# Attention scores over 64 rows per component, on alternating row groups, with unpadded queries and one shared wait

## The chip, the core and the metric

One core of one Trainium2 chip (trn2) runs the whole program. The metric is the device time of one execution in microseconds (us); lower is better. PE is the matrix engine (TensorE), PEld its weight loads, DVE the vector engine, ACT the scalar engine, POOL GpSimd, SP the engine that issues most of the DMAs.

## The reference, cut to what matters

The program is one step of a two-layer decoder: a state-space layer (S5) with GLU and FFN, then differential attention over shared keys and values, and another FFN. The prompt has 1024 positions, the width is 1024, there are 8 heads, and each head has two components of 64 dimensions for queries and keys, and one value of 128. The change touches the attention of the prompt alone:

```python
def diff_attention(q, k, v, q_pos, k_pos, lam):
    s = jnp.einsum("bqhcd,bkhcd->bhcqk", q, k, preferred_element_type=jnp.float32) * (HEAD_DIM ** -0.5)
    mask = k_pos[None, :] <= q_pos[:, None]
    s = jnp.where(mask, s, NEG)
    p = jax.nn.softmax(s, axis=-1)
    w = p[:, :, 0] - lam * p[:, :, 1]
    return jnp.einsum("bhqk,bkhe->bqhe", w.astype(v.dtype), v)
```

Each component c has its own scores and its own softmax; the two are mixed into one weight matrix before the product with the values. Everything is float32.

## The kernel before, in words

The engines run hand-written instruction streams of their own, tied together by semaphores; nothing is reordered by a planner. Attention is 64 steps, numbered c = 0 to 63: head c // 8, query block i = c % 8 of 128 queries. A step works on n = 128 (i + 1) keys, so its size runs from 128 to 1024 within each head. `attention_steps` (L334) unrolls the first and last steps and loops over the rest, on every engine alike.

Data: `kh` holds the keys of a head, component 0 on partitions 0 to 63 and component 1 on partitions 64 to 127, two heads in turn (`par`). `qz` holds the queries twice per head: copy x has component x on its own 64 partitions and zeros on the other 64, so that a contraction over all 128 partitions of `kh` gives the scores of component x alone. The zeros are written once, by two memsets of POOL (L596, L598) before the first head; `load_head` (L459) brings keys and queries by DMA on SP's queue, and waits for `a_o` of the head before.

PSUM: `pair[0]` and `pair[1]` (two banks each) take the scores of component 0 and 1, `pair[2]` the transposes, banks 6 and 7 the outputs.

The order on each engine, in a step with scores c+1:

- PE (`step`, L1723): `scores(c+1, 0)`, `scores(c+1, 1)`, then `outputs(c-2)` (L1701, weights times values), at a head's end `values` (L1678, transposes of the next head's values), then `turn(c-1)` (L1712, transposes of the mixed weights). `scores` (L1686) for component x waits until the exponentials of component x of the step before have read `pair[x]` (`a_exp`), issues one float32 matmul for each 512 keys, and adds the causal mask of the last 128 keys by a bf16 matmul (`identb`, `maskb`), which signals `a_s`. A float32 matmul is two passes in the trace, each with its own weight load.
- DVE (`step`, L1302): `out_copy(c-3)`, the row maximum of component 0 of step c+1 (L1289), reciprocal and factor of step c (L1309, L1312), the mix of step c (L1317, `wmix`), then the row maximum of component 1 of step c+1.
- ACT (`step`, L835): the two exponentials of step c (L841), each of which needs its row maximum and signals `a_exp` after an accumulator read; the eviction of the transposes of step c-2 (L827), at a head's end `v_rows` (L820), the squares of step c-3 (L832).
- POOL and SP work beside it on the sample group's cached keys.

The waits of PE that set the order of the two components:

```python
if c:
    pe.wait_ge(a_exp, v * 2 + (x - 1))
```

Here v is the step's number, so component 0 waits for the first exponential of the step before, and component 1 for the second.

Earlier in the program, the S5 stage has float32 matmuls over 64 rows too (`outputs_s5`, L1530): two such matmuls on one row group, then one over 128 rows, in turn.

Of the kernel before, what the change touches and what calls it, by code (L numbers as in the profile page):

```python
# [20 lines left out]
F32 = mybir.dt.float32  # L21
# [8 lines left out]
P = 128  # L30
DM = 1024
KT = DM // P
SEQ = 1024
# [39 lines left out]
SEG1 = 108  # L73
# [7 lines left out]
def build(nc, d):  # L81
    ctx = ExitStack()
    with ctx:
        top = [((nc.sbuf_base + 31) // 32) * 32]

        def place(name, shape, dt, at=None):

            size = int(np.prod(shape[1:])) * (2 if dt == BF16 else 4)
            size = (size + 31) // 32 * 32
            if at is None:  # L90
                at = top[0]
                top[0] += size
                return nc.alloc_sbuf_tensor_at(name, shape, dt, offset=at)
            off = at[0]
            at[0] += size
            assert at[0] <= at[1], (name, at)
            return nc.alloc_sbuf_tensor_at(name, shape, dt, offset=off)

        def sem(name):
            return ctx.enter_context(nc.semaphore(name))  # L100
# [8 lines left out]
        identb = place("identb", [P, P], BF16)  # L109
# [106 lines left out]

        rf = [ACT_AT, HID_AT]
        kh = place("kh", [P, 2, SEQ], F32, rf)
        qz = place("qz", [P, 2, 2, SEQ], F32, rf)
        vT = nc.alloc_sbuf_tensor_at("vT", [P, 2, SEQ], F32, offset=RAW_AT)  # L220
        vtok = place("vtok", [P, 2, KT, P], F32, rf)
        prob = place("prob", [P, 2, 2, SEQ], F32, rf)
# [67 lines left out]
        d_o, d_sq, d_ssq, d_rs, d_fin = (sem(x) for x in ("d_o", "d_sq", "d_ssq", "d_rs", "d_fin"))  # L290
        op_ready, op_added = sem("op_ready"), sem("op_added")
        d_wp, d_row, d_ot = sem("d_wp"), sem("d_row"), sem("d_ot")
        q_zero, on_r, on_p = sem("q_zero"), sem("on_r"), sem("on_p")
        d_sc, d_hi, d_lo = sem("d_sc"), sem("d_hi"), sem("d_lo")
        passed = sem("passed")
        y_done, y_out = sem("y_done"), sem("y_out")
# [52 lines left out]
        def _(sp):  # L349
# [109 lines left out]
            def load_head(h, par):  # L459
                for c in range(2):  # L460
                    rows = slice(64 * c, 64 * c + 64)
                    for dst, src in ((kh[rows, par, :], k_v), (qz[rows, par, c, :], q_v)):
                        sp.dma_start(dst,
                                     src[ds(h, 1), c, :, :, 0:SEQ].rearrange("o m j t -> (o m) j t")
                                     ).then_inc(hd_in[par], 16)
                sp.dma_start(vT[:, par, :], d["vt"][ds(h, 1), :, 0:SEQ].rearrange("o e t -> (o e) t")
                             ).then_inc(hd_in[par], 16)
# [57 lines left out]
        @block.gpsimd  # L525
        def _(pool):
            g = nc.gpsimd

            def split(u, r, q, first):
                pool.wait_ge(w_in[r], q * 16 + 16)  # L530
                if not first:
                    pool.wait_ge(w_used, u - 2)
                    settle(pool)
                g.tensor_copy(w_hi[:, r, :], w_raw[:, r, :]).then_inc(w_hi_done, 1)  # L534
                pool.wait_ge(w_hi_done, u + 1)
                settle(pool)
                g.tensor_tensor(w_lo[:, r, :], w_raw[:, r, :], w_hi[:, r, :].bitcast(F32), ALU.subtract  # L537
                                ).then_inc(w_split, 1)

            def split_units(first, last):  # L540
                with pool.Fori(first // 4, last // 4) as b:
                    for r in range(4):
                        split(b * 4 + r, r, b, False)


            pool.wait_ge(s5_glob, 1)
            S4 = [P, PP, NI, NJ]
            G4 = [P, PP, NW, 16]
            c = Chain(pool, pool_chain)
            for q in range(PARTS):  # L550
                pr = slice(q * PP, q * PP + PP)
                G_re, G_im = G_r[q % 2], G_i[q % 2]
                if q:
                    pool.wait_ge(s5_h, q)

                def outer(dst, hi_t, lo_t):
                    return g.tensor_tensor(dst[:], bc(hi_t[:, pr, NW + NJ:NN], 3, S4),
                                           bc(lo_t[:, pr, NW:NW + NJ], 2, S4), ALU.mult)

                c.add(outer(CB, cosT, cosT))  # L560
                c.step(outer(CBt, sinT, sinT))
                c.step(g.tensor_tensor(CB[:], CB[:], CBt[:], ALU.subtract))
                c.add(outer(SB, sinT, cosT))
                c.step(outer(CBt, cosT, sinT))
                g.tensor_tensor(SB[:], SB[:], CBt[:], ALU.add).then_inc(s5_cs, 1)
                if q >= 2:
                    pool.wait_ge(s5_y, 8 * (q - 1))

                def cpow(dst, cc, aa):
                    return g.tensor_tensor(dst[:], bc(cc, 2, G4), bc(aa[:, pr, :], 3, G4), ALU.mult)  # L570

                c.add(cpow(G_re, c_in[:, 0, pr, :], A_re))
                c.step(cpow(G_t, c_in[:, 1, pr, :], A_im))
                g.tensor_tensor(G_re[:], G_re[:], G_t[:], ALU.subtract).then_inc(s5_g, 1)
                pool.wait_ge(s5_g, 2 * q + 1)
                c.add(cpow(G_im, ncr[:, pr, :], A_im))
                c.add(cpow(G_t, c_in[:, 1, pr, :], A_re))
                c.sync()
                g.tensor_tensor(G_im[:], G_im[:], G_t[:], ALU.subtract).then_inc(s5_g, 1)
                pool.wait_ge(s5_g, 2 * q + 2)  # L580
                if q == 0:
                    g.memset(ublk[0][:], 0.0).then_inc(s5_zero, 1)
                    pool.wait_ge(u_stored, 16)
                    c.step(g.memset(ublk[1][:], 0.0))
                    g.memset(TM[:], 0.0).then_inc(s5_zero, 1)

            pool.wait_ge(s5_y, 8 * (PARTS - 1))
            pool.wait_ge(s5_k, 4 * PARTS)
            for r in range(4):
                split(r, r, 0, True)  # L590

            split_units(4, SEG1)

            pool.wait_ge(kv_ready, 9 * KT // 2)
            pool.wait_ge(w_split, SEG1)
            g.memset(qz[64:P, :, 0, :], 0.0).then_inc(q_zero, 1)  # L596
            pool.wait_ge(q_zero, 1)
            g.memset(qz[0:64, :, 1, :], 0.0).then_inc(q_zero, 1)  # L598
            pool.wait_ge(q_zero, 2)

            with pool.Fori(0, NS // 2) as bb:
                for par in range(2):
                    for j in range(NPG):
                        if j == 0:
                            pool.wait_ge(kpg_in[0], bb * 64 + (32 * par + 32))
                        else:
                            pool.wait_ge(kpg_in[1], bb * 32 + (16 * par + 16))
                        settle(pool)
                        g.tensor_tensor(kpg[:, j, :], kpg[:, j, :], qb[:, par, :], ALU.mult).then_inc(d_mul, 1)

            pool.wait_ge(on_r, 1)
            for h in range(6):
                g.tensor_tensor(O[:, h], O[:, h], bc(orst[:, 8 * h:8 * h + 8], 2, [P, KT, P]), ALU.mult
                                ).then_inc(on_p, 1)
            split_units(SEG1, N_UNITS)
# [801 lines left out]
        def _(pe):  # L1417
            t_ = nc.tensor

            def mm(out, lhsT, rhs, start, stop):  # L1420
                return t_.matmul(out, lhsT, rhs, start=start, stop=stop)  # L1421
# [261 lines left out]
                    last = t_.transpose(pair[2][:, kb * P:(kb + 1) * P], vT[:, par, kb * P:(kb + 1) * P], ident[:])  # L1683
                last.then_inc(a_vt, 1)

            def scores(v, c, x):  # L1686

                i, par = c % 8, (c // 8) % 2
                if c % 8 == 0:
                    pe.wait_ge(hd_in[par], v * 5 + (80 * (c // 16 + 1) - 5 * c))  # L1690
                if c:
                    pe.wait_ge(a_exp, v * 2 + (x - 1))
                q = qz[:, par, x, i * P:(i + 1) * P]
                n = (i + 1) * P
                for at in range(0, n, 512):
                    end = min(at + 512, n)
                    last = mm(pair[x][:, at:end], q, kh[:, par, at:end], True, end < n)
                last = mm(pair[x][:, n - P:n], identb[:], maskb[:], False, True)
                last.then_inc(a_s, 1)

            def outputs(v, h, c):  # L1701

# [19 lines left out]

            def step(v, h, c):  # L1723
                if c != 63:
                    scores(v + 1, c + 1, 0)
                    scores(v + 1, c + 1, 1)
                if c >= 2:
                    outputs(v - 2, h if c % 8 >= 2 else h - 1, c - 2)
                if c % 8 == 7 and c != 63:
                    values(v + 1, h + 1, c + 1)  # L1730
                if c >= 1:
                    turn(v - 1, h + (2 if c % 8 == 7 and c != 63 else 1), c - 1)


            pe.wait_ge(kv_evicted, 9 * KT)
            pe.wait_ge(q_zero, 2)
            values(0, 0, 0)
            scores(0, 0, 0)
            scores(0, 0, 1)
            pe.wait_ge(d_qrow, 1)  # L1740
            attention_steps(pe, step)
            outputs(62, 7, 62)
# [179 lines left out]
```

## Time and profile before

| what | value |
|---|---|
| median of 3 executions | 2925.18 us (2923.54 to 2928.95) |
| profiled execution, first to last instruction (span) | 2914.3 us |
| PE busy in the span | 2601.8 us (89%) |
| DVE, ACT, POOL busy | 1225.4, 539.8, 801.2 us |
| attention of the prompt | about 1650 to 1952 us |

The profile gives no time of its own for the profiled execution beside the span. The span lies 10.9 us below the median, which is what lies around the first and the last instruction and the difference between executions. A timeline row gives the start, the duration, the engine and line, the operation with its output and inputs, and in brackets how long the engine had been idle before it and what released it. The end of a matmul is modelled, so its duration holds some latency, and starts are the better guide to how fast passes follow each other. PEclk is the clock that was granted to TensorE: 1.00 is 2.4 GHz, 0.50 is 1.2 GHz.

### The profile page before, as it was taken

How to read it: one execution, taken by the hardware profiler on the slowest of the kernel's cores; microseconds unless marked ns; L12 is line 12 of the kernel's file. 1: busy time of each engine (PE TensorE's matmuls, PEld its weight loads, DVE VectorE, ACT ScalarE, POOL GpSimd, SP SyncE). 2: the span in 40 equal slices, each digit the busy share in tenths (PEclk: the TensorE clock that was granted, in tenths of full speed). 3: DMA queues.
4: the chain of work that ended last, by engine and by line, in shares of the span. 5: the costliest groups of instructions: out<-in, count | busy, mean ns of one | idle time of the engine just before them, and what ended most of it. 6: DMA issues, size and time to landing. Idle time of an engine off the chain costs nothing.

```text
span 2914.3 us, 41251 instructions
## 1 busy us (share of the span) xinstructions
PE 2601.8 (89%) x16204; PEld 2460.8 (84%) x16204; DVE 1225.4 (42%) x2126; ACT 539.8 (19%) x1188; POOL 801.2 (27%) x439
## 2 busy tenths in 40 slices
PE   0468879999999999998999788879999999999997
PEld 0356679999999999998999566657999999999997
DVE  7876032433333333338114276663443333333237
ACT  2111131220000000003112255542120000000002
POOL 4163112223222332223323201130223232222230
PEclk9966589999999999999999899999999999999998
DMA  2423321111111111111322233223111111111101
GB/s 83 96 33 43 86 94 50 38 38 56 45 44 44 46 51 50 45 44 51 109 87 73 95 88 80 78 80 117 51 37 49 44 54 44 44 44 44 45 29 59
DMA packets 78896, 173.95 MB, mean 60 GB/s; under 512 B 18762, under 2 KB 41546, under 8 KB 78674
## 3 DMA queue, kind: packets, MB, share of 16 engines
q1 hardware_dynamic: 74994, 157.84, 18.6%
q10 hardware_dynamic: 3744, 13.74, 1.2%
q8 instruction: 131, 2.15, 0.3%
q14 instruction: 27, 0.22, 0.0%
HBM read 143.51 MB, written 25.69 MB: 58 GB/s over the span
## 4 chain that ended last, share of the span: by engine, by line
PE 82%; DVE 11%; issue 3%; DMA 2%; ACT 1%; SPq 1%; DVEq 0%; ACTq 0%
PE pair L1421 80%; DVE acc L913 2%; DVE act_lo L913 1%; DVE nmx L1289 1%; PE pair L1719 1%; DMA u<-U 1%; DVE tmp L941 1%; DVE X L913 0%; DVE diag L935 0%; DVE rho L1312 0%; DVE bbar L913 0%; DVE U L1081 0%; SPq L431 0%; DMA vT<-vt 0%; DVE wmix L1317 0%
## 5 line engine op out<-in xcount | busy, mean ns | idle before, releaser
L1421 PE MATMUL pair<-act_hi,w_hi 128*128 128x344 f32 x3264 | 1053.3, 323 | 43.8 <-DVE act_lo L913 33.8
L1421 PE MATMUL pair<-act_lo,w_hi 128*128 128x344 f32 x3264 | 1050.1, 322 | 8.3 <-issue 8.3
L1421 PE MATMUL pair<-act_hi,w_lo 128*128 128x344 f32 x3264 | 1049.8, 322 | 0.0
L1421 PEld LDWEIGHTS pair<-act_hi,w_hi 128*128 128x128 f32 x3264 | 621.6, 190 | 47.5 <-issue 36.1
L534 POOL CAST w_hi<-w_raw 128x1024 fp32r<-128x1024 f32 x180 | 196.0, 1089 | 1589.0 <-PE pair L1421 819.9
L1421 PEld LDWEIGHTS pair<-act_lo,w_hi 128*128 128x128 f32 x3264 | 619.6, 190 | 9.4 <-issue 9.4
L1421 PEld LDWEIGHTS pair<-act_hi,w_lo 128*128 128x128 f32 x3264 | 620.5, 190 | 0.0
L537 POOL TENSOR_TENSOR w_lo<-w_raw,w_hi 128x1024 fp32r<-128x1024 f32 x180 | 433.9, 2411 | 32.4 <-POOL w_hi L534 32.4
L913 DVE TENSOR_TENSOR tmp<-gate,pair 128x344 f32<-128x344 f32 x132 | 67.8, 513 | 762.8 <-ACT gate L745 762.8
L913 DVE TENSOR_TENSOR X<-X,pair 128x344 f32<-128x344 f32 x552 | 270.5, 509 | 199.8 <-PE pair L1421 199.7
L1421 PE MATMUL pair<-hid_lo,w_hi 128*128 128x344 f32 x1056 | 337.9, 320 | 0.0
L1421 PE MATMUL pair<-hid_hi,w_lo 128*128 128x344 f32 x1056 | 337.8, 320 | 0.0
L1421 PE MATMUL pair<-hid_hi,w_hi 128*128 128x344 f32 x1056 | 337.3, 319 | 0.0
L745 ACT ACTIVATE gate<-pair 128x344 f32<-128x344 f32 x132 | 60.4, 458 | 1200.0 <-PE pair L1421 1200.0
L1421 PEld LDWEIGHTS pair<-hid_hi,w_hi 128*128 128x128 f32 x1056 | 198.8, 188 | 0.0
L1421 PEld LDWEIGHTS pair<-hid_lo,w_hi 128*128 128x128 f32 x1056 | 198.5, 188 | 0.0
L1421 PEld LDWEIGHTS pair<-hid_hi,w_lo 128*128 128x128 f32 x1056 | 198.3, 188 | 0.0
L913 DVE TENSOR_TENSOR hid_lo<-tmp,hid_hi 128x344 fp32r<-128x344 f32 x132 | 164.7, 1248 | 73.7 <-ACT hid_hi L747 73.7
L1421 PE MATMUL pair<-kh,qz 128*128 128x512 f32 (+3 forms) x384 | 153.7, 521 | 30.4 <-ACT prob L841 29.4
L1421 PEld LDWEIGHTS pair<-kh,qz 128*128 128x128 f32 x384 | 65.6, 198 | 83.1 <-issue 54.3
L1289 DVE TENSOR_REDUCE nmx<-pair 128x1 f32<-128x256 f32 (+7 forms) x128 | 96.4, 753 | 76.8 <-PE pair L1421 76.7
L841 ACT ACTIVATE prob<-pair,nmx 128x256 f32<-128x256 f32 (+7 forms) x128 | 94.6, 740 | 95.8 <-DVE nmx L1289 94.8
(222 smaller groups left out, 2120.6 us busy)
## 6 DMA issues: line engine op xcount, KB each, us to landing
w_raw<-w SPq DMA_DIRECT2D x180, 512.0 KB, 3.5
kpg<-cache_k SPq DMA_DIRECT2D x16, 512.0 KB, 9.3
vpg<-cache_v SPq DMA_DIRECT2D x16, 512.0 KB, 4.2
X<-x_t SPq DMA_DIRECT2D x3, 1376.0 KB, 10.3
vt<-stage ACTq DMA_DIRECT2D x8, 516.0 KB, 4.7
y_t<-Y SPq DMA_DIRECT2D x3, 1376.0 KB, 5.4
ublk<-u SPq DMA_DIRECT2D x32, 128.0 KB, 5.2
z<-zblk SPq DMA_DIRECT2D x32, 128.0 KB, 3.3
```

The lines of the kernel that those rows point to most:

```text
L534: g.tensor_copy(w_hi[:, r, :], w_raw[:, r, :]).then_inc(w_hi_done, 1)
L537: g.tensor_tensor(w_lo[:, r, :], w_raw[:, r, :], w_hi[:, r, :].bitcast(F32), ALU.subtract).then_inc(w_split, 1)
L745: a.activation(gate[:, n, :], bank[2 * n][:, 0:CW], ACT.Silu).then_inc(gu_silu, 1)
L841: a.activation(prob[:, c % 2, x, 0:n], pair[x][:, 0:n], ACT.Exp, bias=nmx[:, c % 2, x:x + 1], accum_out=sums[:, c % 2, x:x + 1]).then_inc( ...
L913: return v_.tensor_tensor(out, a, b, op)
L941: return v_.scalar_tensor_tensor(out, view(X[:, k, cols]), gains[:, g, k:k + 1], view(R[:, cols]), ALU.mult, ALU.mult)
L1289: v_.tensor_reduce(nmx[:, c_ % 2, x:x + 1], pair[x][:, 0:n], axis=AXX, op=ALU.max, negate=True).then_inc(a_max, 1)
L1421: return t_.matmul(out, lhsT, rhs, start=start, stop=stop)
L1719: last = t_.transpose(pair[2][:, kb * P:(kb + 1) * P], wmix[:, c % 2, kb * P:(kb + 1) * P], ident[:])
```

## The change

The padded queries `qz` become `qh`, in the layout of `kh`: each component on its own 64 partitions, once. The two memsets and the semaphore `q_zero` with PE's wait for it go away. `scores` does both components in one call: it waits once, until both exponentials of the step before are done, then issues for each chunk of up to 512 keys the matmul of component 0 over partitions 0 to 63 and that of component 1 over partitions 64 to 127, and after all chunks the two mask matmuls, each of which signals `a_s`. The number of DMAs, the other engines' orders and their waits stay.

```diff
-        qz = place("qz", [P, 2, 2, SEQ], F32, rf)
+        qh = place("qh", [P, 2, SEQ], F32, rf)
...
-                    for dst, src in ((kh[rows, par, :], k_v), (qz[rows, par, c, :], q_v)):
+                    for dst, src in ((kh[rows, par, :], k_v), (qh[rows, par, :], q_v)):
...
-            pool.wait_ge(kv_ready, 9 * KT // 2)
-            pool.wait_ge(w_split, SEG1)
-            g.memset(qz[64:P, :, 0, :], 0.0).then_inc(q_zero, 1)
-            pool.wait_ge(q_zero, 1)
-            g.memset(qz[0:64, :, 1, :], 0.0).then_inc(q_zero, 1)
-            pool.wait_ge(q_zero, 2)
...
-            def scores(v, c, x):
+            def scores(v, c):
 
                 i, par = c % 8, (c // 8) % 2
                 if c % 8 == 0:
                     pe.wait_ge(hd_in[par], v * 5 + (80 * (c // 16 + 1) - 5 * c))
                 if c:
-                    pe.wait_ge(a_exp, v * 2 + (x - 1))
-                q = qz[:, par, x, i * P:(i + 1) * P]
+                    pe.wait_ge(a_exp, v * 2)
                 n = (i + 1) * P
                 for at in range(0, n, 512):
                     end = min(at + 512, n)
-                    last = mm(pair[x][:, at:end], q, kh[:, par, at:end], True, end < n)
-                last = mm(pair[x][:, n - P:n], identb[:], maskb[:], False, True)
-                last.then_inc(a_s, 1)
+                    for x in range(2):
+                        rows = slice(64 * x, 64 * x + 64)
+                        mm(pair[x][:, at:end], qh[rows, par, i * P:(i + 1) * P], kh[rows, par, at:end], True, end < n)
+                for x in range(2):
+                    mm(pair[x][:, n - P:n], identb[:], maskb[:], False, True).then_inc(a_s, 1)
...
                 if c != 63:
-                    scores(v + 1, c + 1, 0)
-                    scores(v + 1, c + 1, 1)
+                    scores(v + 1, c + 1)
...
-            pe.wait_ge(q_zero, 2)
             values(0, 0, 0)
-            scores(0, 0, 0)
-            scores(0, 0, 1)
+            scores(0, 0)
```

## Rows read from the trace of the kernel before

**Rows 1.** Page, costliest groups: scores, row maxima and exponentials.
```profile
L1421 PE MATMUL pair<-kh,qz 128*128 128x512 f32 (+3 forms) x384 | 153.7, 521 | 30.4 <-ACT prob L841 29.4
L1289 DVE TENSOR_REDUCE nmx<-pair 128x1 f32<-128x256 f32 (+7 forms) x128 | 96.4, 753 | 76.8 <-PE pair L1421 76.7
L841 ACT ACTIVATE prob<-pair,nmx 128x256 f32<-128x256 f32 (+7 forms) x128 | 94.6, 740 | 95.8 <-DVE nmx L1289 94.8
```

**Rows 2.** Busy time by window over the attention: PE, PEld, DVE, ACT, POOL, clock, DMA.
```profile
1648.00:1952.20 304.20, 263.35 (x1383) 181.18 (x1383) 214.21 (x395) 167.98 (x449) 56.42 (x26) 0.95 0.29 87
```

**Rows 3.** Instructions by line, 1648 to 1950 us: the mix.
```profile
L1317 DVE SCALAR_TENSOR_TENSOR wmix<-prob,rho 128x128 f32<-128x128 f32 (+7 forms) x63 | 57.0, 905 | 2.5
```

**Rows 4.** Waits between engines, 1648 to 1950 us: total, times, longest.
```profile
ACT prob L841 <- DVE nmx L1289: 92.5, 87, 4.2
DVE nmx L1289 <- PE pair L1421: 76.7, 50, 14.8
...
PE pair L1421 <- ACT prob L841: 29.4, 26, 3.1
```

**Rows 5.** Timeline of one step with 896 keys and the next.
```profile
1820.24 1.09 DVE L1289 TENSOR_REDUCE nmx<-pair 128x1 f32<-128x896 f32 x1 [1.32 <-PE pair L1421]
...
1821.70 1.02 DVE L1317 SCALAR_TENSOR_TENSOR wmix<-prob,rho 128x768 f32<-128x768 f32 x1
...
1822.63 1.08 DVE L1289 TENSOR_REDUCE nmx<-pair 128x1 f32<-128x896 f32 x1
...
1823.15 1.88 PE L1421 MATMUL pair<-kh,qz 128*128 128x512 f32 x4
...
1823.75 1.01 ACT L841 ACTIVATE prob<-pair,nmx 128x896 f32<-128x896 f32 x1 [1.28 <-DVE nmx L1289]
...
1824.65 0.19 ACT L841 ACTIVATION_READ_ACCUMULATOR prob<-pair,nmx 128x1 f32 x1
...
1824.87 0.22 PE L1421 MATMUL pair<-maskb,identb 128*128 128x128 bf16 x1
...
1824.92 1.96 PE L1421 MATMUL pair<-kh,qz 128*128 128x512 f32 x4
1825.12 1.23 DVE L1289 TENSOR_REDUCE nmx<-pair 128x1 f32<-128x1024 f32 x1 [1.15 <-PE pair L1421]
```

**Rows 6.** Timeline at the end of that head.
```profile
1828.83 0.22 PE L1421 MATMUL pair<-maskb,identb 128*128 128x128 bf16 x1
...
1831.65 0.77 PE L1421 MATMUL pair<-kh,qz 128*128 128x128 f32 x2 [2.60 <-ACT prob L841]
...
1832.32 2.76 PE L1421 MATMUL pair<-vtok,wT 128*128 128x128 f32 x12
...
1837.79 0.21 ACT L841 ACTIVATION_READ_ACCUMULATOR prob<-pair,nmx 128x1 f32 x1
```

**Rows 7.** Busy time by window around the gap in rows 6.
```profile
1828.06:1831.48 3.42, 0.98 (x10) 0.76 (x8) 2.66 (x4) 1.18 (x3) 0.00 (x0) 0.99 0.00 0
1831.48:1834.89 3.41, 3.24 (x15) 3.16 (x16) 1.87 (x4) 0.72 (x2) 0.00 (x0) 0.51 0.00 0
```

**Rows 8.** Timeline of PE in the S5 outputs.
```profile
346.05 0.82 PE L1421 MATMUL pair<-ublk,TM 128*128 128x136 f32 x2
346.80 0.82 PE L1421 MATMUL pair<-H,G_re 64*128 64x136 f32 x2
...
348.00 0.59 PE L1421 MATMUL pair<-ublk,TM 128*128 128x136 f32 x1
```

**Rows 9.** Busy time by window in the S5 outputs.
```profile
332.00:360.00 28.00, 28.00 (x87) 20.73 (x87) 0.00 (x0) 2.78 (x7) 13.35 (x8) 0.50 0.43 162
```

**Rows 10.** Timeline of the first head's start: a memset, and PE's first transposes.
```profile
1631.73 1.80 POOL L598 MEMSET qz<- 64x2048 f32 x1
...
1647.98 1.94 PE L1683 MATMUL pair<-ident,vT 128*128 128x128 f32 x8 [15.16 <-DMA vT<-vt]
```

More of the change, by code:

```diff
@@ L292, in build @@
         d_wp, d_row, d_ot = sem("d_wp"), sem("d_row"), sem("d_ot")
-        q_zero, on_r, on_p = sem("q_zero"), sem("on_r"), sem("on_p")
+        on_r, on_p = sem("on_r"), sem("on_p")
         d_sc, d_hi, d_lo = sem("d_sc"), sem("d_hi"), sem("d_lo")
```

## The prediction

> **What bounds the kernel now.** I read the page's groups first, then the busy times of the attention stage, the waits between engines there, and the timeline of one head. The scores are 384 passes [rows 1]; outside the attention nothing changes, so the question is about the 302 us from 1650 to 1952, or 37.8 us for each of the 8 heads. In that stage PE is busy 87% of the time and DVE 70% [rows 2], which looks like a stage that PE bounds. But the waits run in a ring: ACT waits 92.5 us for row maxima, DVE 76.7 us for scores, PE 29.4 us for exponentials [rows 4]. The timeline shows why PE is still well fed. The passes of component 0 with 1024 keys start at 1823.15, while the second exponential of the step before runs from 1823.75; those of component 1 start at 1824.92, just after that exponential was read out at 1824.84. Then DVE takes the first maximum (1825.12) beside component 1's passes [rows 5]. The two components work in turns: PE on one, DVE and ACT on the other. The two waits, one for each component, are what allows it.
>
> **The ring after the change.** Now both components wait for the second exponential of the step before, and both masks, whose signals release the maxima, come after all chunks. So nothing of a step's scores lies beside the maxima and exponentials of the step before, and the ring is closed once in a step: scores of both, maximum 0, factor and mix of the step before, maximum 1, exponential 1, and back. Outputs and transposes, 16 passes in the largest step, lie beside DVE's part.
>
> Its length without the passes: from maximum 0 (1820.24) to the release of the next component's passes (1824.92) is 4.68 us for 896 keys, of which 1.09 + 1.02 + 1.08 + 1.01 are the two maxima, the mix and the exponential, and 0.48 are the rest [rows 5]. From the start of four passes (1823.15) to the maximum (1825.12) is 1.97; the passes take 1.72 of it, as the mask that follows starts at 1824.87. That leaves 0.25 for mask and signal, and makes one pass of 512 columns 0.43 us. So a step has 0.73 us of fixed parts. For the seven steps of a head with 256 keys and more:
> - maxima: 96.4 / 8 = 12.05 us per head, less two of about 0.28 for 128 keys [rows 1] = 11.5;
> - mixes: 57.0 / 8 = 7.1 [rows 3], less that of 1024 keys, which falls into the next head's first step (1.3, estimated from 1.02 for 768 keys), = 5.8;
> - exponentials of one component: 94.6 / 16 = 5.9 [rows 1], less 0.4 = 5.5;
> - fixed: 7 x 0.73 = 5.1.
>
> Together 27.9 us. A head's first step goes another way: the outputs, the transposes of new values and `v_rows` stand ahead of its exponentials. It takes now from 1831.65 to the next release at about 1838.1, 6.4 us [rows 6], and goes on as it is, since the new passes (128 keys) are short. **A head without passes of its other seven steps: 34.3 us**, against 37.8 with everything now. This is the number that decides.
>
> **The passes.** A float32 matmul is two passes. Written so, the queue has component 0 first and second, then component 1 first and second, then the next chunk. If a pass can run beside one of the other row group but passes start in order, only the second of one pair lies beside the first of the next: one chunk takes 3 pass times where it took 4, two full chunks 5 where they took 8. For 256 to 1024 keys, with 0.43 us for 512 columns: 0.64, 0.96, 1.28, 1.49, 1.71, 1.92, 2.13 = 10.1 us per head. One after another it would be 14.9, and as two full halves 7.5; no row shows two row groups at once, so these are the bounds. I take the middle form, because in the trace passes always start in order.
>
> The Trainium skill (TensorE: Matmul & The Clock Gate, Part 3) says that matmuls on different row groups run at the same time, starting about 4 ns apart; by it as it stands, the sum would go by the 7.5, which is 2.6 us per head or 21 us in all below mine. No run so far shows it.
>
> **The change between 64 and 128 rows.** S5 is the nearest place: there a cycle of four passes over 64 rows and two over 128, 136 columns each, takes 348.00 - 346.05 = 1.95 us [rows 8] at the half clock [rows 9]. Six such passes are 6 x 0.227 = 1.36 (136/512 of 0.43, doubled). So two changes cost 0.59 us at 1.2 GHz. Each score step gets two (into the 64 rows, back for the mask). The clock may scale all of it or none, 0.3 to 0.6 a step; at the full clock I take 0.3: 7 x 0.3 = 2.1 us per head.
>
> The Trainium skill (TensorEngine Tiling (Array Packing), Key Properties) says that a change of tiling mode drains TensorE. It speaks against this change, and the trace agrees, with 0.59 us for two.
>
> **At the full clock**: 34.3 + 10.1 + 2.1 = 46.5 us, 8.7 more than 37.8, for 8 heads **70 us** more.
>
> **The clock.** Now PE has one long gap in a head, 2.60 us from 1829.05 to 1831.65 [rows 6], and the granted clock falls from 0.99 to 0.51 right behind it, for the next 3.4 us [rows 7]. After the change the ring leaves PE a gap in every step. With 1024 keys DVE's and ACT's part is 5.2 us and outputs and transposes about 2.0; the gap is 3.2. With 512 keys it is 3.4 less 0.7, or 2.7. So five steps of each head (512 keys and more) have a gap at least as long as the one that costs the clock today. And mixed passes over 64 rows did not bring it back in S5: 28 us with PE marked busy throughout, at 0.50 [rows 9]. I take half clock for the passes from 640 keys up (+7.25), half of that for 512 (+0.64), 0.3 for changes and masks in each of five steps (+1.5), and about as much for the slower small steps (+1.5): 10.9 us per head, **87 us**. Outputs and transposes at half clock (3.4 us for the largest) still fit beside DVE's part.
>
> **Nothing or next to nothing.** The memsets took 1.80 us each on POOL, done at 1633.5, while PE waited for the first values until 1647.98 [rows 10]: no gain, the DMA covers it. Loads keep their number, bytes and waits; a longer stage gives them more time. Fewer waits on PE save nothing where PE waits anyway.
>
> **Sum**: 70 + 87 = 157 us. Against the span 2914.3 that is 3071; the median lies 10.9 above the span, and nothing around it changes, so **3083 us**.
>
> **The rivals.**
> - *The row groups run one after another* (the array takes no second row group, or the instruction does not ask for it: the change does not do what it says). For it: no row shows two row groups at once. Against it: weight loads already run beside passes (PE and PEld together are busy for longer than the stage) [rows 2], so the array does take work in parts. The Trainium skill's rule above speaks against it too. The time: 34.3 + 14.9 + 2.1 = 51.3 at full clock, plus a clock term of 12.8 for the passes of five steps and 3 for the rest: 67, 29 more per head, 234 in all: about 3160. Chance 0.15.
> - *The clock holds.* If the gaps are broken by late outputs, PE stays at 2.4 GHz and the change costs the ring alone: 70 us, or with full concurrency 49: 2974 to 2995. For it: 0.95 granted now [rows 2]; against it: five gaps as long as the one that dropped it. Chance 0.16.
> - *PE was the bound, and the change relieves it.* 15.4 us of passes per head (with 128 keys) fall to 10.5 or 7.7, less 8 x 0.3 for changes: 2.5 to 5.3 saved per head, 20 to 42 in all, about 2895. It decides only if the ring is shorter than PE's work, that is if the part without passes is under 37.8 - 10.1 - 2.1 = 25.6 us per head. It is 34.3, so even passes of no length would win only 1.4 us per head after the changes. Chance 0.03, and 0.01 for a time that cannot be told from now.
> - The forecast, ring plus clock, has 0.65; its own range is 3040 to 3130, from full concurrency (34.3 + 7.5 + 2.1 + about 8, or 51.9 per head, +113) to half clock in all steps (+16 per head for the clock, +198).
>
> The range for 8 in 10 is 2990 to 3165: it leaves out the faster rival, the lower part of the second one and the upper part of the first. A measurement of this kernel can tell about 0.2% from no change; faster by more than that 0.03, within it 0.01, slower 0.96.
>
> **What would show it.** The profile after should show: PE's passes of both components starting after the read of the second exponential, never beside it; maximum 0 starting only after both components' passes; DVE and PE idle in turn, with PE's share in the stage well under 87%; a period of 8 to 10 us with 1024 keys, where a step now takes under 5 on average; component 1's first pass starting with component 0's second; a granted clock of 0.6 to 0.8 over the stage; and a stage of about 460 us in place of 302. Passes that start all one after another make the first rival true, a clock above 0.9 the second. I am wrong altogether if maximum 0 starts before component 1's last pass, which would mean that the two components still work in turns.

## The result, and the profile after

| kernel | median | runs | against before (95% interval) |
|---|---|---|---|
| before | 2925.78 us | 2923.54 to 2928.95 | |
| changed | 3006.77 us | 3003.06 to 3013.87 | 1.0281 (1.0263 to 1.0300) |

The change costs 81 us. The forecast was 3083, with a range of 2990 to 3165: the sign and the mechanism hold, the size is half of what was forecast, and 3007 lies below the 3040 to 3130 that the prediction gave for ring and clock as it had sized them. The profiled execution has a span of 3001.2 us, 86.9 more than before. Its time is 1.9 us above its span; so most of the 10.9 us that lie between span and median before are no fixed part: the execution profiled before was one of the fastest.

The groups that answer to [rows 1], from the page of the changed kernel:

```profile
L1414 PE MATMUL pair<-kh,qh 64*128 64x512 f32 (+3 forms) x384 | 109.6, 690 | 123.5 <-ACT prob L834 123.5
L1282 DVE TENSOR_REDUCE nmx<-pair 128x1 f32<-128x256 f32 (+7 forms) x128 | 96.4, 754 | 182.5 <-PE pair L1414 182.5
```

The 384 passes are busy for 109.6 us in place of 153.7: the two row groups overlap, as the starts of the passes show further down. But the idle time ahead of them grew from 30.4 to 123.5 us, all of it waiting for exponentials. The maxima take what they took (96.4) and wait 182.5 us in place of 76.8.

The stage by the window view, which answers to [rows 2] (PE, PEld, DVE, ACT, POOL, clock, DMA):

```profile
1648.00:2038.00 390.00, 254.18 (x1383) 168.63 (x1383) 208.39 (x395) 167.30 (x447) 55.78 (x26) 0.81 0.24 69
```

It ends 86 us later. PE is busy for 254 us, 9 less than before, in a stage that is much longer: 65% of it in place of 87%. DVE has 208 of 390. No engine is near its limit. The granted clock is 0.81 on the mean, where it was 0.95; the prediction expected 0.6 to 0.8, and a stage of about 460 us.

Waits between engines in that stage, which answer to [rows 4]:

```profile
DVE nmx L1282 <- PE pair L1414: 182.5, 64, 17.0
ACT prob L834 <- DVE nmx L1282: 172.7, 102, 5.3
...
PE pair L1414 <- ACT prob L834: 123.5, 50, 7.0
```

All three edges of the ring are longer, PE's more than four times. This is the ring that the prediction described. In the timeline, the step with 1024 keys that answers to [rows 5]:

```profile
1833.02 0.19 ACT L834 ACTIVATION_READ_ACCUMULATOR prob<-pair,nmx 128x1 f32 x1
...
1833.27 2.58 PE L1414 MATMUL pair<-kh,qh 64*128 64x512 f32 x8 [1.86 <-ACT prob L834]
...
1835.78 0.40 PE L1414 MATMUL pair<-maskb,identb 128*128 128x128 bf16 x2
...
1835.97 2.28 PE L1414 MATMUL pair<-vtok,wT 128*128 128x128 f32 x10
1836.11 1.22 DVE L1282 TENSOR_REDUCE nmx<-pair 128x1 f32<-128x1024 f32 x1 [3.77 <-PE pair L1414]
...
1837.70 1.15 DVE L1310 SCALAR_TENSOR_TENSOR wmix<-prob,rho 128x896 f32<-128x896 f32 x1
...
1838.76 1.22 DVE L1282 TENSOR_REDUCE nmx<-pair 128x1 f32<-128x1024 f32 x1
...
1840.02 1.11 ACT L834 ACTIVATE prob<-pair,nmx 128x1024 f32<-128x1024 f32 x1 [1.44 <-DVE nmx L1282]
...
1841.27 0.77 PE L1414 MATMUL pair<-kh,qh 64*128 64x128 f32 x4 [2.37 <-ACT prob L834]
```

Read it as a chain. The second exponential of the step before is read out at 1833.21, the passes of both components follow at 1833.27, maximum 0 comes after all of them (DVE had been idle for 3.77 us), then the mix, maximum 1, exponential 1, and the next passes at 1841.27. One turn of the ring is 8.00 us; over the heads, turns of this size take 7.35 us where the clock stays up and up to 9.21 where it does not. No pass lies beside an exponential of its own ring, and in the 2.37 us before 1841.27 PE has nothing to do.

### The profile page after: what moved, and what is told of

The parts are those of the page before. It is cut to its first block, busy times and chain, and to the rows that moved or that the text cites. A ratio compares the mean times of both kernels' runs of the same rounds, so it can differ in the third digit from the quotient of the medians.

```text
span 3001.2 us, 41241 instructions
## 1 busy us (share of the span) xinstructions
PE 2592.1 (86%) x16204; PEld 2448.3 (82%) x16204; DVE 1219.3 (41%) x2126; ACT 540.2 (18%) x1188; POOL 796.9 (27%) x437
## 4 chain that ended last, share of the span: by engine, by line
PE 79%; DVE 12%; issue 4%; DMA 2%; ACT 2%; SPq 1%; DVEq 0%; ACTq 0%
PE pair L1414 78%; DVE nmx L1282 3%; DVE acc L906 1%; DVE act_lo L906 1%; DMA u<-U 1%; DVE wmix L1310 1%; DVE tmp L934 0%; DVE rho L1305 0%; PE pair L1713 0%; DVE X L906 0%; DVE diag L928 0%; DVE bbar L906 0%; ACT prob L834 0%; SPq L431 0%; DVE U L1074 0%
## 5 line engine op out<-in xcount | busy, mean ns | idle before, releaser
L1414 PE MATMUL pair<-kh,qh 64*128 64x512 f32 (+3 forms) x384 | 109.6, 690 | 123.5 <-ACT prob L834 123.5
L1414 PEld LDWEIGHTS pair<-kh,qh 64*128 64x128 f32 x384 | 40.8, 236 | 164.1 <-ACT prob L834 132.8
L1282 DVE TENSOR_REDUCE nmx<-pair 128x1 f32<-128x256 f32 (+7 forms) x128 | 96.4, 754 | 182.5 <-PE pair L1414 182.5
L602 POOL TENSOR_TENSOR kpg<-kpg,qb 128x1024 f32<-128x1024 f32 x16 | 37.2, 2349 | 348.1 <-DMA kpg<-cache_k 348.1
```

The source lines that it names most:

```text
L1282: v_.tensor_reduce(nmx[:, c_ % 2, x:x + 1], pair[x][:, 0:n], axis=AXX, op=ALU.max, negate=True).then_inc(a_max, 1)
```

## The experiments

Times and ratios are each kernel's own against the kernel before on the same chip. The kernels were timed on several chips, where the kernel before has medians of 2923.5 to 2925.8 us, so a difference between two of them holds some 2 us of that.

A time is for the whole program, and part of what separates these kernels lies behind the attention, in instructions that no edit touches. The changed kernel and the one with work in PE's gaps, each split by the window view (columns as in [rows 2]) at the last pass of the attention's outputs:

```profile
1652.20:2050.20 398.00, 260.54 (x1433) 174.81 (x1432) 210.83 (x400) 171.98 (x457) 55.78 (x26) 0.82 0.23 66
2050.20:3001.20 951.00, 906.65 (x5767) 893.84 (x5765) 348.52 (x602) 116.45 (x236) 240.24 (x140) 0.97 0.16 51
```

```profile
1652.00:2024.20 372.20, 290.00 (x1573) 172.27 (x1572) 212.62 (x400) 171.97 (x457) 56.25 (x26) 0.94 0.25 70
2024.20:2958.10 933.90, 896.83 (x5767) 884.67 (x5765) 348.56 (x602) 116.43 (x236) 240.52 (x140) 0.98 0.16 52
```

The same 5767 passes follow the attention in both, and take 17 us less in the second. In the feed-forward stage behind the attention of the first, PE pauses four times, for 1.6 to 2.1 us, where nothing in the profile holds it back ("issue"), and the clock falls to half at each pause. The kernel before has such pauses too; this is the first, from its timeline:

```profile
2305.14 0.42 PE L1421 MATMUL pair<-act_lo,w_hi 128*128 128x344 f32 x1 [2.06 <-issue]
```

Seven of the twelve kernels have all four, five have none. It goes with the kernel, not with the chip: the seven have the same number of passes in the attention (1433), the five have more or fewer. Whether that decides it, and how, is open. So what an edit does to the attention is read from this table, one trace for each kernel; the execution profiled of the kernel before was one of its fastest, so up to 10 us of a distance to it can be the difference between executions.

| kernel | attention, first pass of scores to last of outputs (us) | behind it (us) | pauses |
|---|---|---|---|
| before | 315.0 | 949.6 | 4 |
| changed | 398.0 | 951.0 | 4 |
| own waits back | 354.1 | 949.9 | 4 |
| shared wait alone | 371.6 | 949.3 | 4 |
| all but the row groups | 480.5 | 946.5 | 4 |
| both maxima first | 322.7 | 948.1 | 4 |
| work in PE's gaps | 372.2 | 933.9 | 0 |
| component after component | 394.4 | 944.1 | 4 |
| without the masks | 388.1 | 933.2 | 0 |
| both maxima first, small filler | 317.9 | 928.1 | 0 |
| the same, padded queries | 355.4 | 928.0 | 0 |
| the same, component after component | 320.0 | 929.8 | 0 |

**Own waits back, 64 rows kept.**

```diff
-            def scores(v, c):
+            def scores(v, c, x):
...
-                    pe.wait_ge(a_exp, v * 2)
+                    pe.wait_ge(a_exp, v * 2 + (x - 1))
+                rows = slice(64 * x, 64 * x + 64)
...
-                for x in range(2):
-                    mm(pair[x][:, n - P:n], identb[:], maskb[:], False, True).then_inc(a_s, 1)
+                mm(pair[x][:, n - P:n], identb[:], maskb[:], False, True).then_inc(a_s, 1)
```

> The changed kernel with its unpadded 64-row passes, but the two components one after the other again, each with its own wait and its mask right behind it. Theory (the shared wait and the masks behind both components close a ring in every step): the turns come back, PE works on one component while DVE and ACT work on the other, and maximum 0 starts beside the passes of component 1. What stays is two more changes of row mode a step on a PE that was 87% busy: 2935 to 2975 us. Rival (what costs is the 64-row mode itself, its changes and a lower clock): there are twice as many changes here, so it stays at 3007 or goes above it.

Measured 2957.07 us, ratio 1.0117 (1.0098 to 1.0136): 50 us less than the change, in the range of the theory. Both components, 512 keys, PE's timeline:

```profile
1829.14 1.12 PE L1414 MATMUL pair<-kh,qh 64*128 64x512 f32 x2
1830.20 0.23 PE L1414 MATMUL pair<-maskb,identb 128*128 128x128 bf16 x1
1830.36 1.12 PE L1414 MATMUL pair<-kh,qh 64*128 64x512 f32 x2
1831.41 0.23 PE L1414 MATMUL pair<-maskb,identb 128*128 128x128 bf16 x1
1831.48 0.44 PE L1414 MATMUL pair<-vtok,wT 128*128 128x128 f32 x2
```

Two passes of 512 columns take 2 x 0.43 = 0.86 us at the full clock, and the masks start 1.06 and 1.05 us behind the first of them: 0.2 us for the change from 64 to 128 rows. The other way, the pass starts 0.16 us behind the mask, where passes over 128 rows start 0.05 us behind it [rows 5]: 0.11 us for the change back. The turns are back. What stays of the loss, 31 us, has the size of the changes, 64 steps with two of each or 40 us at most, on a PE that had little to spare; but the granted clock is lower too (0.86 from 1648 to 1952 us, where it was 0.95), and no run parts the two.

**The shared wait alone, on the kernel before.**

```diff
                 if c:
-                    pe.wait_ge(a_exp, v * 2 + (x - 1))
+                    pe.wait_ge(a_exp, v * 2)
```

> The kernel before, padded queries over 128 rows and component after component, with one edit: component 0 waits for both exponentials too. Theory: maximum 0 can still start beside the passes of component 1, so only the passes of one component enter the ring: 34.3 + 7.5 = 41.8 us a head against 37.8, 32 us, and up to 30 more for the clock: 2957 to 2990. Rival (the wait is harmless, it is the order of the masks or the row groups): 2926 to 2935.

Measured 2976.44 us, ratio 1.0185 (1.0161 to 1.0208). One number in one wait costs 51 us. From its waits:

```profile
DVE nmx L1289 <- PE pair L1421: 148.1, 67, 15.8
...
PE pair L1421 <- ACT prob L841: 83.1, 44, 4.5
```

PE's wait for exponentials grows from 29.4 us [rows 4] to 83.1, with no row group and no change of order in sight.

**All of the change but the row groups.** Padded queries, one shared wait, chunks in turn, masks last. The order of the chunks, from the edit:

```diff
                 for at in range(0, n, 512):
                     end = min(at + 512, n)
-                    last = mm(pair[x][:, at:end], q, kh[:, par, at:end], True, end < n)
+                    for x in range(2):
+                        mm(pair[x][:, at:end], qz[:, par, x, i * P:(i + 1) * P], kh[:, par, at:end], True, end < n)
```

> The kernel before with everything of the change but the row groups: one shared wait, chunks of the two components in turn, both masks last, over 128 padded rows. Theory: both components' passes enter the ring, one after another: 34.3 + 14.9 = 49.2 us a head, 91 us, and up to 30 for the clock: 3015 to 3050. The distance to 3007 is what the concurrency of the row groups gives back, less their changes of mode. Rival (concurrency gives nothing): 3007 or less.

Measured 3078.2 us, ratio 1.0524 (1.0503 to 1.0546), above what was expected. The sign is right: holding both masks back puts the second component's passes into the ring too, 102 us more than the shared wait alone. The size is not, and the timeline says why. The step with 896 keys:

```profile
1800.59 6.16 PE L1421 MATMUL pair<-kh,qz 128*128 128x512 f32 x8 [5.34 <-ACT prob L841]
1806.58 0.28 PE L1421 MATMUL pair<-maskb,identb 128*128 128x128 bf16 x2
```

Eight passes, 4 x (0.43 + 0.32) = 3.0 us at the full clock, take 5.99: they run at half clock throughout, behind a gap of 5.34 us. This is one of the slowest of its size: in the eight heads it takes 3.11 to 6.13 us. What lies in the ring pays for the clock too: from first pass to mask, the seven larger steps take 177 us in all, where the full clock would give 125. Against this kernel the row groups give back 71 us.

**DVE takes both maxima first.**

```diff
                 if c_ != 63:
                     row_max(v + 1, c_ + 1, 0)
+                    row_max(v + 1, c_ + 1, 1)
...
-                if c_ != 63:
-                    row_max(v + 1, c_ + 1, 1)
```

> The changed kernel with one edit on DVE: both row maxima of a step come first, then reciprocal, factor and mix of the step before. Theory: the mix (5.8 us a head) and reciprocal and factor (0.37 for each of 7 steps) leave the ring, 8.4 us a head, 67 us: about 2940, and down to 2910 if the shorter gaps leave the clock alone. Rival (PE's work, not DVE's order, sets the step): within 10 us of 3007.

Measured 2925.79 us, ratio 1.0009 (0.9998 to 1.0019): 81 us less than the change, all of the loss, without touching PE. From its timeline, the step with 1024 keys:

```profile
1800.36 1.99 PE L1413 MATMUL pair<-kh,qh 64*128 64x512 f32 x8 [1.76 <-ACT prob L834]
...
1802.28 0.29 PE L1413 MATMUL pair<-maskb,identb 128*128 128x128 bf16 x2
...
1802.73 2.34 DVE L1282 TENSOR_REDUCE nmx<-pair 128x1 f32<-128x1024 f32 x2
...
1805.11 1.11 ACT L834 ACTIVATE prob<-pair,nmx 128x1024 f32<-128x1024 f32 x1
...
1805.44 1.15 DVE L1311 SCALAR_TENSOR_TENSOR wmix<-prob,rho 128x896 f32<-128x896 f32 x1
...
1806.37 0.49 PE L1413 MATMUL pair<-kh,qh 64*128 64x128 f32 x4 [1.98 <-ACT prob L834]
```

The mix now runs beside the second exponential (1805.44 beside 1805.11), and the turn of the ring is 6.01 us in place of 8.00. The fastest turns of this size, with the clock up in both kernels, are 5.83 and 7.35 us: the 1.52 between them are the mix with its reciprocal and factor (1.15 + 0.37). The rest of the 2 us here is mostly the clock (8 passes in 1.92, against 2.51).

**Work in PE's gaps.**

```diff
                 if c:
+                    pe.wait_ge(a_exp, v * 2 - 1)
+                    for _ in range((0, 0, 0, 1, 2, 2, 2, 2)[(c - 1) % 8]):
+                        mm(pair[0][:, 0:512], ident[:], kh[:, ((c - 1) // 8) % 2, 0:512], True, True)
                     pe.wait_ge(a_exp, v * 2)
```

> The changed kernel with work put into PE's gaps: after the first exponential of a step, and before the wait for the second, one or two float32 matmuls of 512 columns into pair[0] (identity times keys, overwritten by the next scores) in the steps behind 512 keys and more. They fit beside the second exponential. Theory (part of the loss is the clock, which falls in these gaps): the granted clock of the stage rises from 0.81 towards 0.95, and the time falls by 15 to 35 us, to 2972 to 2992. Rival (the clock costs nothing here, since the passes it slows are not in the ring): the clock rises and the time stays at 3007 or goes up.

Measured 2959.77 us, ratio 1.0127 (1.0107 to 1.0147). PE does more work, none of it useful, and the program is 47 us faster, more than was expected. The window from 1700 to 1850 us of this kernel:

```profile
1700.00:1850.00 150.00, 119.13 (x684) 71.76 (x682) 88.35 (x175) 74.28 (x204) 13.96 (x6) 0.99 0.27 71
```

The clock is 0.99 there; in the changed kernel it is 0.85 in the same window. But 17 of the 47 us lie behind the attention, where the four pauses are gone. In the attention itself the filler brings 26 us (398.0 to 372.2), which is inside the 15 to 35 that were expected, and 23 of them are in the passes: from the first pass of scores to the mask, the seven larger steps of all heads take 101 us in the changed kernel and 78 here. So of the 81 us the clock costs at least 26 by the traces, about 30 by the times, and the ring the other 50 or so. At 0.94 the clock of this attention is that of the kernel before (0.94 from 1649.7 to 1964.7 us).

**Component after component, wait and masks as in the change.**

```diff
-                for at in range(0, n, 512):
-                    end = min(at + 512, n)
-                    for x in range(2):
-                        rows = slice(64 * x, 64 * x + 64)
+                for x in range(2):
+                    rows = slice(64 * x, 64 * x + 64)
+                    for at in range(0, n, 512):
+                        end = min(at + 512, n)
```

> The changed kernel with all chunks of component 0 ahead of those of component 1, everything else as it is. Up to 512 keys nothing changes. Theory (passes of the two row groups run side by side where they are near each other in the queue): from 640 keys up only part of the passes still overlap, 0.6 to 1.3 us more a step, 4 us a head, 25 to 35 us in all: 3030 to 3045. Rival (the queue looks far enough ahead for any order): 3007.

Measured 2997.61 us, ratio 1.0260 (1.0239 to 1.0282). The theory falls: there is no loss, in the time or in the attention (394.4 us against 398.0). With 1024 keys:

```profile
1831.56 1.99 PE L1414 MATMUL pair<-kh,qh 64*128 64x512 f32 x8 [3.15 <-ACT prob L834]
1833.48 0.29 PE L1414 MATMUL pair<-maskb,identb 128*128 128x128 bf16 x2
```

Four passes of component 0 stand ahead of four of component 1 in the program, and all eight take 1.92 us: four pass times and 0.2 for the change of mode. Each row group works through its own passes. Alternating the chunks, as the change does, is not needed for it. The ratio lies 0.2% below that of the change, with intervals that overlap; 7 us of the distance lie behind the attention.

**Without the masks.** The kernel leaves out the masking, and the last passes carry the signals:

```diff
-                for x in range(2):
-                    mm(pair[x][:, n - P:n], identb[:], maskb[:], False, True).then_inc(a_s, 1)
...
+                        if end == n:
+                            ins.then_inc(a_s, 1)
```

> The changed kernel without the mask matmuls, so the scores above the diagonal are not masked; the last passes signal the maxima themselves. Theory (the change from 64 to 128 rows stands in the ring at the mask, about 0.2 us, with 0.1 for the masks): 0.2 to 0.35 us a step, 13 to 22 us in all: 2985 to 2995. Rival (the change of mode is hidden, or it only moves to the outputs behind): within 5 us of 3007.

Measured 2976.32 us, ratio 1.0186 (1.0163 to 1.0209): 30 us less than the change, more than expected; but 18 of them lie behind the attention, where the four pauses are gone. In the attention it is 10 us. The fastest turns of a size are 0.16 to 0.18 us shorter (384 keys 3.57 against 3.75, 640 keys 5.02 against 5.20, 1024 keys 7.18 against 7.35), and 0.17 us in each of 63 turns make 11 us. That is at the lower edge of what was expected of the change of mode and the masks together.

**Both maxima first, and a small filler.** The DVE order of the fourth experiment, and on PE:

```diff
+                    pe.wait_ge(a_exp, v * 2 - 1)
+                    if (c - 1) % 8 >= 4:
+                        mm(pair[0][:, 0:384], ident[:], kh[:, ((c - 1) // 8) % 2, 0:384], True, True)
                     pe.wait_ge(a_exp, v * 2)
```

> The version with both maxima first on DVE (2925.8), and one float32 matmul of 384 columns into pair[0] after the first exponential in the steps behind 640 keys and more. Theory (the clock still falls in its gaps): the clock of the stage rises from 0.88, and the time falls below both kernels, 2905 to 2922. Rival: the filler delays the scores where the clock is low, 2925 to 2940.

Measured 2899.68 us, ratio 0.9918 (0.9902 to 0.9933): the fastest program, 24 us below the kernel before and 107 below the change, 5 us below the band that was expected. The same window as above:

```profile
1700.00:1850.00 150.00, 123.46 (x741) 81.07 (x740) 107.46 (x197) 82.68 (x224) 18.64 (x8) 0.93 0.31 84
```

0.93, where the version without the filler has 0.87. But the gain does not come from there. In the attention the filler brings 5 us (322.7 to 317.9), and the attention is no faster than it was before the change (315.0, in a fast execution); 20 of the 24 to 26 us lie behind it, where this kernel has none of the four pauses. The clock did rise, as the theory has it, but that this makes the attention faster than in the kernel before is not shown.

**Are the row groups needed for that time?** The same version with the padded queries (and the memsets that they need):

```diff
-                        rows = slice(64 * x, 64 * x + 64)
-                        mm(pair[x][:, at:end], qh[rows, par, i * P:(i + 1) * P], kh[rows, par, at:end], True, end < n)
+                        mm(pair[x][:, at:end], qz[:, par, x, i * P:(i + 1) * P], kh[:, par, at:end], True, end < n)
```

> The fastest version so far (both maxima first, filler, 2899.7) with the padded 128-row queries in place of the row groups. Theory (in a ring the concurrency of the row groups counts in full): the seven larger steps of a head take 14.9 us of passes in place of 7.5, less about 0.2 us for each of 8 changes of mode that go away: 5.8 us a head, 46 us: 2940 to 2955, slower than the kernel before. Rival (the gain comes from DVE's order and the filler alone): 2900 to 2915.

Measured 2936.19 us, ratio 1.0036 (1.0022 to 1.0049): slower than the kernel before, 37 us above the version with row groups, and all of it in the attention (355.4 us against 317.9; behind it both take 928). The direction is as the theory has it; the expected band began at 2940.

**Is the chunk order needed?** The 2899.7 us version, component after component:

```diff
-                for at in range(0, n, 512):
-                    end = min(at + 512, n)
-                    for x in range(2):
-                        rows = slice(64 * x, 64 * x + 64)
+                for x in range(2):
+                    rows = slice(64 * x, 64 * x + 64)
+                    for at in range(0, n, 512):
+                        end = min(at + 512, n)
```

> The fastest version so far (2899.7) with all chunks of component 0 ahead of those of component 1. The chunk by chunk order made no loss when it was undone in the changed kernel (2997.6 against 3006.8). If that order matters at all, this lies 2 to 10 us below 2899.7; if it was the difference between chips, within 3 us of it.

Measured 2902.31 us, ratio 0.9926 (0.9905 to 0.9947): no difference that can be told.

## Why the prediction was right, and where not

- **The ring: right, and shown.** Restoring the two waits takes away 50 of the 81 us. Setting the shared wait alone makes 51 us, and taking the mix out of the ring takes all 81 away, with the same number of pauses behind the attention in all of these kernels. The fixed part was well sized. The step with 640 keys, at the full clock, from the changed kernel's timeline:

```profile
1859.79 1.35 PE L1414 MATMUL pair<-kh,qh 64*128 64x512 f32 x8 [2.62 <-ACT prob L834]
...
1861.07 0.29 PE L1414 MATMUL pair<-maskb,identb 128*128 128x128 bf16 x2
...
1865.07 1.95 PE L1414 MATMUL pair<-kh,qh 64*128 64x512 f32 x4 [2.88 <-ACT prob L834]
```

  The turn is 5.28 us. By the prediction's parts it would be 0.73 + 2 x 0.81 + 0.75 + 0.80 + 1.49 + 0.3 = 5.69. The passes with their change of mode take 1.28 of it where the prediction has 1.79, which is more than the whole difference; the fixed parts are 0.1 above it.

- **The passes: mis-sized.** The step that failed is "passes start in order", which gave 1.49 us here and 10.1 a head. Measured are 1.28 from the first pass to the masks, which is 2 x (0.43 + 0.11) = 1.07 for passes wholly side by side (half the serial 2.13) and 0.21 for the change of mode. By the starts, from the changed kernel's timeline of PE (512 keys, a moment in the first passes and a later one):

```profile
1855.33 0.70 PE L1414 MATMUL pair<-kh,qh 64*128 64x512 f32 x2 [0.41 <-ACT prob L834]
...
1855.86 0.60 PE L1414 MATMUL pair<-kh,qh 64*128 64x512 f32 x2
```

  Two passes start together, and the next two together half a microsecond later. A row group does not wait for the other one's second pass. The lower bound of 7.5 us a head was the true value, 21 us of the miss. Here the Trainium skill (TensorE: Matmul & The Clock Gate, Part 3) was the better guide: matmuls on different row groups run at the same time, and the trace agrees, 8 passes in 4 pass times.

- **The change of mode: right.** 0.3 us a step at the full clock was taken from S5's 0.59 for two at half clock. The first experiment shows 0.20 into 128 rows and 0.11 back. In the ring only the first one stands, because PE is idle ahead of the passes.

- **The clock: right in kind, about three times too large.** 87 us were forecast; the filler shows 26 in the attention, 30 by the times. The failed step is "half clock for the passes from 640 keys up", laid on passes that were themselves too long, with another 3 us a head for changes, masks and small steps. Windows of the changed kernel, columns as in [rows 2]:

```profile
1862.20:1865.61 3.41, 0.54 (x2) 0.38 (x4) 2.00 (x5) 2.36 (x7) 0.00 (x0) 0.95 1.06 180
1865.61:1869.02 3.41, 3.41 (x16) 1.90 (x13) 0.88 (x2) 0.08 (x1) 0.00 (x0) 0.55 0.95 341
1869.02:1872.44 3.42, 0.77 (x8) 0.54 (x6) 2.38 (x6) 2.19 (x5) 1.84 (x1) 0.95 0.28 115
1872.44:1875.85 3.41, 3.41 (x12) 1.32 (x12) 0.02 (x1) 0.57 (x3) 2.80 (x2) 0.55 0.00 0
```

  The clock falls behind the gap and is back in the stretch after the busy one, though the busy one is mostly passes over 64 rows. It alternates, and does not stay down. Here both busy stretches get the low clock, and so it goes in most heads: from the first pass to the mask, 768 keys take 2.5 to 2.9 us in six heads of eight (1.49 at the full clock), 896 keys 3.0 to 3.3 in six (1.71), and 640 keys 2.2 to 2.4 in five (1.28). The largest step, with 1024 keys, is at the full clock in four heads (1.92) and wholly at half in one (3.72). The seven larger steps of all heads take 101 us, where the full clock would give 72: 29 us, for which the prediction had 63. The gaps were sized well behind 512 keys (2.62 us against 2.7), and too long behind 1024 (2.37 us against 3.2). The S5 rows [rows 9], where passes over 64 rows stayed at 0.50 for 28 us, were the wrong comparison: there each pair of passes was split by changes of mode. But no run here tells which difference to S5 matters.

- **The sum.** With the passes and the change of mode put right, the ring at the full clock is 34.3 + 7.5 + 7 x 0.2 = 43.2 us a head; the fastest turns of each size in the filled kernel, the first head left out, add up to 42.4. Against 37.8 that is 43 us in all, and the clock 26 to 30: some 71, where 81 were measured. The 10 us that are left lie in single longer turns and were not taken apart; in the filled kernel, for one, the mix of 768 keys at 1772.10 takes 3.07 us where it takes 1.02 elsewhere. The forecast had 70 and 87 for the same two terms (and its last addition, 2914.3 + 157 + 10.9, gives 3082, not 3083).

- **The rivals.** The row groups side by side refute the first. The clock did not hold (0.81), so not the second; but its price, the ring alone for 49 to 70 us, is nearer to the 81 than the forecast's 157 is, and 3007 lies between the two. The third, that PE was the bound and is relieved, is refuted by the changed kernel itself: PE's share fell to 65% and the time rose.

## What to carry to other kernels

Before two waits become one, draw the ring: which engine's part of step c now stands between two turns, and what lay beside it before. A faster stage of a ring gives its gain only if the others' order lets it, and the cheapest repair can be on another engine: here moving one instruction on DVE was worth 81 us. It brought the attention back to about what it was, not below. Where a ring leaves PE gaps of two or three microseconds in every turn, the clock has a price of its own, and the passes in the ring pay it: here 26 to 30 of 81 us. And before a gain is credited to an edit, split the span at the end of the edited stage: the version that beats the kernel before by 24 us has 21 of them, by its trace, behind the attention, in a stage that the edit did not touch.

## What the runs showed of the hardware that was not expected

- Float32 matmuls over 64 rows on two row groups overlap completely, in whatever order the program has them: 8 passes of 512 columns in 1.92 us, of which 0.2 are the change of mode, with chunks in turn or component after component.
- A change from passes over 64 rows to one over 128 costs 0.20 us, the way back 0.11 us, at the full clock (own waits back).
- Useless matmuls can make a stage faster: 70 of them (140 passes of 512 columns) brought 26 us in the attention, by a granted clock of 0.94 in place of 0.82.
- Four pauses of PE with nothing in the profile to hold it back, 1.6 to 2.4 us each in the feed-forward stage behind, most of them with a fall of the clock to half, come and go with edits elsewhere in the program. The part behind the attention takes 944 to 951 us with them and 928 to 934 without. Why they come is open.
